# A decoder trunk on one core: rows of each norm split between two engines, the memory's load and norm put in among the first projections

## What is computed

```python
mem_n = rms_norm(mem, mem_norm)               # 256 x 1024, once
for l in range(2):
    h = rms_norm(x, norm_mix[l])
    p = h @ w_in[l]                           # one wide projection for three mixers
    ...                                       # RWKV-7, gated DeltaNet, sparse MLA
    x = x + (g_a * y_a + g_b * y_b + g_c * y_c) @ w_mix_out[l]
    x = x + memory_xattn(rms_norm(x, norm_xattn[l]), mem_n, ...)
    h = rms_norm(x, norm_ffn[l])
    x = x + (swiglu(h, ...) if l == 0 else moe_swiglu(h, router, ...))
return rms_norm(x, final_norm)

def rms_norm(x, g):
    return x * rsqrt(mean(x * x, -1) + eps) * g
```

## Time and profile before

| | us |
|---|---|
| three runs, median | 3019.67 |
| three runs, lowest and highest | 3012.88, 3020.87 |
| profiled execution, own time | 3020.0 |
| profiled execution, span of the core | 3017.8 |
| PE busy | 2599.6 |
| DVE busy | 1691.3 |
| ACT busy | 1452.7 |
| mean granted clock of TensorE | 0.949 |

### The profile page before, as it was taken

The page is one execution under the profiler, slowest core; times in us unless marked ns, Lnnn a source line. Parts: engine busy times, 40 slices in busy tenths (PEclk is TensorE's granted clock), DMA queues, the critical chain, the costliest instruction groups (busy, mean ns, idle before and its releaser), DMA issues.

```text
span 3017.8 us, 67151 instructions
## 1 busy us (share of the span) xinstructions
PE 2599.6 (86%) x29799; PEld 2135.1 (71%) x29818; DVE 1691.3 (56%) x1990; ACT 1452.7 (48%) x1904; POOL 353.8 (12%) x180
## 2 busy tenths in 40 slices
PE   6988888899788989888988997878888888888887
PEld 5766666777466768666756875657787788878876
DVE  2445453234215532545542343149999989999996
ACT  2233343233224321433343323248887878888785
POOL 0000001000000000000010000002322322332231
PEclk9999999999999999899989999989999999999999
DMA  5401030133217634211120232249999999999994
GB/s 183 147 29 57 21 94 29 37 101 105 94 56 256 205 105 136 71 43 30 57 70 23 80 109 84 98 175 385 373 354 363 363 354 368 357 362 365 354 366 183
DMA packets 304032, 531.34 MB, mean 176 GB/s; under 512 B 18528, under 2 KB 145760, under 8 KB 303360
## 3 DMA queue, kind: packets, MB, share of 16 engines
q1 hardware_dynamic: 303600, 525.99, 50.4%
q10 hardware_dynamic: 144, 1.05, 0.1%
HBM read 524.91 MB, written 2.10 MB: 175 GB/s over the span
## 4 chain that ended last, share of the span: by engine, by line
PE 64%; DVE 16%; ACT 12%; issue 7%; DMA 0%; ACTq 0%; POOL 0%; DVEq 0%; SPq 0%
PE bank L797 11%; PE bank L698 9%; DVE arena L2680 8%; PE bank L1368 6%; PE bank L1385 4%; PE bank L768 4%; PE bank L1268 4%; PE bank L1227 4%; ACT arena L1989 4%; PE bank L763 3%; PE bank L716 2%; PE bank L642 2%; PE bank L1412 2%; PE bank L1284 2%; DVE yacc L2688 2%
## 5 line engine op out<-in xcount | busy, mean ns | idle before, releaser
L2680 DVE TENSOR_TENSOR arena<-ring,arena 128x2048 bf16<-128x2048 f32 x336 | 813.9, 2441 | 81.9 <-ACT arena L1989 81.9
L1989 ACT ACTIVATE arena<-ring 128x2048 bf16<-128x2048 f32 x336 | 630.4, 1907 | 0.0
L1368 PE MATMUL bank<-arena 128*128 128x0 bf16 x10752 | 489.0, 209 | 42.8 <-DVE arena L2680 32.6
L1368 PEld LDWEIGHTS bank<-arena 128*128 128x128 bf16 x10752 | 478.7, 99 | 49.0 <-DVE arena L2680 35.7
L797 PE MATMUL bank<-feat,ring 128*128 128x256 f32 x1664 | 436.6, 401 | 8.4 <-ACT ring L1554 2.3
L1518 POOL TENSOR_TENSOR arena<-yacc,arena 128x512 bf16<-128x512 f32 x112 | 296.5, 2647 | 1060.2 <-ACT arena L2012 1060.2
L797 PEld LDWEIGHTS bank<-feat,ring 128*128 128x128 f32 x1664 | 310.0, 197 | 88.2 <-issue 43.5
L1385 PEld LDWEIGHTS bank<-arena 128*128 128x128 bf16 x5376 | 254.9, 102 | 15.8 <-issue 10.5
L1385 PE MATMUL bank<-arena 128*128 128x0 bf16 x5376 | 260.2, 212 | 1.2 <-DVE arena L2680 1.1
L698 PE MATMUL bank<-feat,ring 128*128 128x256 f32 x1056 | 230.7, 381 | 5.8 <-issue 5.8
L698 PEld LDWEIGHTS bank<-feat,ring 128*128 128x128 f32 x1056 | 201.6, 191 | 34.7 <-issue 7.1
(11 more groups left out here) (353 smaller groups left out, 3382.1 us busy)
## 6 DMA issues: line engine op xcount, KB each, us to landing
ring<-in_moe_w_gate SPq DMA_DIRECT2D x112, 1024.0 KB, 7.0
ring<-in_moe_w_up SPq DMA_DIRECT2D x112, 1024.0 KB, 6.5
ring<-in_moe_w_down SPq DMA_DIRECT2D x112, 1024.0 KB, 7.0
ring<-in_w_in SPq DMA_DIRECT2D x76, 1024.0 KB, 5.2
ring<-in_xa_w_kv SPq DMA_DIRECT2D x16, 1024.0 KB, 5.4
ring<-in_ffn_w_gate SPq DMA_DIRECT2D x11, 1024.0 KB, 5.3
ring<-in_ffn_w_up SPq DMA_DIRECT2D x11, 1024.0 KB, 5.4
ring<-in_ffn_w_down SPq DMA_DIRECT2D x11, 1024.0 KB, 6.9
```

The lines of the kernel that those rows point to most:

```text
L1368: m = mm(o, w[k // 4][wi][:, k % 4, col:col + P], xg[:, e % 2, xi, k, :].shape_from_register(width[e % 2]), start=i == 0 and k == 0, stop= ...
L1989: sc.activation(w_parts[b][0], ring[:, b * FFN_SLOT:(b + 1) * FFN_SLOT], ACT.Copy).then_inc(S["w_hi"], 1)
L2680: v.tensor_tensor(w_parts[b][1], ring[:, b * FFN_SLOT:(b + 1) * FFN_SLOT], w_parts[b][0], ALU.subtract).then_inc(S["w_lo"], 1)
```

## The change

It has three parts.

Each of the seven norms whose result is turned now splits the scaling: ACT writes `xn` for `t` = 0 (a Copy with the row's factor as its scale), DVE only for `t` = 1. PE turns the eight blocks of half 0 once ACT's is done, and then the eight of half 1. A bank is full when its last block of half 1 is in. The final norm is as it was.

The loads are in another order: `mem` is issued behind the second chunk of `w_in`, `rout` behind the fourth and with a semaphore of its own, for which PE waits only at the router (L1318 of the changed kernel). ACT, DVE and PE wait at the start for `par` and `cs` alone.

The memory's norm is taken from the start and put behind the first two chunks (four tiles) of layer 0's projections, on all three engines. PE does not wait there for its eight results, but later, behind the twelfth chunk.

```diff
@@ SP
             sp.dma_start(par[:, :, :], params.rearrange("l p n -> p l n")).then_inc(S["par_dma"], 16)
-            sp.dma_start(yacc[...], mem...).then_inc(S["mem_dma"], 16)
             sp.dma_start(xt[:, :, :], x.rearrange("(a p) d -> p a d", p=P)).then_inc(S["in_dma"], 16)
             sp.dma_start(cs[:, :], consts).then_inc(S["par_dma"], 16)
-            sp.dma_start(rout[:, :, :], rows(router)).then_inc(S["par_dma"], 16)
...
                 for i, ch in enumerate(mix_chunks(l)):
+                    if not l and i == 2:
+                        sp.dma_start(yacc[...], mem...).then_inc(S["mem_dma"], 16)
+                    if not l and i == MIX_SLOTS:
+                        sp.dma_start(rout[:, :, :], rows(router)).then_inc(S["rout_dma"], 16)
@@ PE
-            def norm():
-                pe.wait_ge(S["norm_xn"], c.need("norm_xn", 2))
-                for b in range(4):
-                    for k in (2 * b, 2 * b + 1):
-                        for t in range(TT):
-                            m = tr(bk(4 + b, (k % 2) * 256 + t * P, P), xn[:, t, k * P:(k + 1) * P])
-                            if not k and not t:
-                                release(m)
-                            if k % 2 and t == 1:
-                                m.then_inc(S["norm_T"], 1)
-                pe.wait_ge(S["feat_ready"], c.need("feat_ready", 4))
-                pe.wait_ge(S["feat_half"], c.need("feat_half", 4))
+            def norm(used=True):
+                for t, done in enumerate(("norm_x0", "norm_xn")):
+                    pe.wait_ge(S[done], c.need(done))
+                    for k in range(KT):
+                        m = tr(bk(4 + k // 2, (k % 2) * 256 + t * P, P), xn[:, t, k * P:(k + 1) * P])
+                        if not k and not t:
+                            release(m)
+                        if k % 2 and t == 1:
+                            m.then_inc(S["norm_T"], 1)
+                if used:
+                    pe.wait_ge(S["feat_ready"], c.need("feat_ready", 4))
+                    pe.wait_ge(S["feat_half"], c.need("feat_half", 4))
...
-                proj_chunks(12, feat)
+                if l:
+                    proj_chunks(12, feat)
+                else:
+                    proj_chunks(2, feat)
+                    norm(False)
+                    proj_chunks(10, feat)
+                    pe.wait_ge(S["feat_ready"], c.need("feat_ready", 4))
+                    pe.wait_ge(S["feat_half"], c.need("feat_half", 4))
...
             def moe_route():
+                pe.wait_ge(S["rout_dma"], 16)
...
-            pe.wait_ge(S["par_dma"], c.need("par_dma", 48))
-            norm()
+            pe.wait_ge(S["par_dma"], c.need("par_dma", 32))
@@ ACT
+                act.wait_ge(S["norm_r"], c.need("norm_r"))
+                act.wait_ge(*c.last())
+                sc.activation(xn[:, 0, :], src[:, 0, :], ACT.Copy, scale=small[:, 6:7]).then_inc(*c.inc("norm_x0"))
...
                     evac(raw[:, n % 4, 3:259])
+                    if not l and n == 3:
+                        act.wait_ge(S["mem_dma"], 16)
+                        norm(yflat.rearrange("p (a b) -> p a b", a=TT), "mem_norm", 0, memf)
...
-            act.wait_ge(S["par_dma"], 48)
+            act.wait_ge(S["par_dma"], 32)
             sc.activation(small[0:1, 78:79], par[0:1, 0, 0:1], ACT.Copy).then_inc(*c.inc("act_step"))
-            act.wait_ge(S["mem_dma"], 16)
-            norm(yflat.rearrange("p (a b) -> p a b", a=TT), "mem_norm", 0, memf)
@@ DVE
-                for t in range(TT):
+                for t in range(TT) if final else (1,):
...
                     v.scalar_tensor_tensor(dst, dst, pc(l, "mu", n), raw[:, n % 4, 3:259], ALU.mult, ALU.add).then_inc(*c.inc("raw_free"))
+                    if not l and n == 3:
+                        dve.wait_ge(S["mem_dma"], 16)
+                        norm(yflat.rearrange("p (a b) -> p a b", a=TT), "mem_norm", 0, memf)
```

More of the change, by code:

```diff
@@ L89 @@
 SEMS = ("in_dma par_dma mem_dma wl_dma slot0 slot1 slot2 slot3 slot4 slot5 weights_used "
-        "dve_step act_step norm_ss norm_ms norm_sd norm_xn norm_T feat_ready feat_half x_new "
+        "dve_step act_step norm_ss norm_ms norm_sd rout_dma norm_xn norm_x0 norm_r norm_T feat_ready feat_half x_new "
         "proj_full proj_evac raw_free gate_sig rkv_ready vlow_full vlow vres_full vres_sig vres_done "
@@ L548, in _ @@
             sp.dma_start(par[:, :, :], params.rearrange("l p n -> p l n")).then_inc(S["par_dma"], 16)
-            sp.dma_start(yacc[:, :, :].rearrange("p a b -> p (a b)").rearrange("p (a d) -> p a d", a=TT),
-                         mem.rearrange("(a p) d -> p a d", p=P)).then_inc(S["mem_dma"], 16)
             sp.dma_start(xt[:, :, :], x.rearrange("(a p) d -> p a d", p=P)).then_inc(S["in_dma"], 16)
             sp.dma_start(cs[:, :], consts).then_inc(S["par_dma"], 16)
-            sp.dma_start(rout[:, :, :], rows(router)).then_inc(S["par_dma"], 16)
             def load(chunk, slots, rounds=0):
@@ L592, in _ @@
                 for i, ch in enumerate(mix_chunks(l)):
+                    if not l and i == 2:
+                        sp.dma_start(yacc[:, :, :].rearrange("p a b -> p (a b)").rearrange("p (a d) -> p a d", a=TT),
+                                     mem.rearrange("(a p) d -> p a d", p=P)).then_inc(S["mem_dma"], 16)
+                    if not l and i == MIX_SLOTS:
+                        sp.dma_start(rout[:, :, :], rows(router)).then_inc(S["rout_dma"], 16)
                     if i == MIX_SLOTS:
@@ L624, in _ @@
             load_moe(down_chunks(NE * STEPS - 1, NE - 1))
-            sp.wait_ge(S["norm_xn"], 2 * (2 + 3 * LAYERS))
+            sp.wait_ge(S["norm_xn"], 1 + 3 * LAYERS + TT)
             sp.dma_start(out.rearrange("(a p) d -> p a d", p=P),
@@ L2133, in norm @@
                 dve.wait_ge(S["norm_sd"], c.need("norm_sd"))
-                v.reciprocal(small[:, 6:8], small[:, 4:6]).then_inc(*c.inc("dve_step"))
+                v.reciprocal(small[:, 6:8], small[:, 4:6]).then_inc(*c.inc("dve_step" if final else "norm_r"))
                 dve.wait_ge(*c.last())
-                for t in range(TT):
+                for t in range(TT) if final else (1,):
                     if final:
                         if t == 0:
-                            dve.wait_ge(S["par_dma"], 64)
+                            dve.wait_ge(S["par_dma"], 48)
                         v.scalar_tensor_tensor(yflat[:, t * D:(t + 1) * D], src[:, t, :], small[:, 6 + t:7 + t],
@@ L2749, in moe @@
                 dve.wait_ge(S["mo_x"], 4 * NE)
-            dve.wait_ge(S["par_dma"], 48)
-            dve.wait_ge(S["mem_dma"], 16)
-            norm(yflat.rearrange("p (a b) -> p a b", a=TT), "mem_norm", 0, memf)
+            dve.wait_ge(S["par_dma"], 32)
             dve.wait_ge(S["in_dma"], 16)
```

## The result

The changed kernel takes 3024.14 us (median of 22 runs) against 3019.55 for the kernel before (median of 22 runs beside them): ratio 1.0017, 95% interval 1.0011 to 1.0024. It is slower by 0.17%, 4.6 us. One of the 22 executions of the changed kernel took 10095.91 us; the ratio leaves it out, and without it the median is 3024.07. The prediction was 3018.9 us, 0.75 faster, with a range of 3011 to 3025. The time lies inside the range, but on the other side of the kernel before, and the interval does not reach down to 1. The forecast of a small gain was wrong.

The account below looks back on a forecast made before the run. Bound: the opening's chain of loads and norms until 34 us, then PE. Terms -3.0 - 9.35 + 10.1 + 0.3 + 1.2 = -0.75 took the median of 3019.67 to 3018.9 us, range 3011 to 3025.

Parts of the forecast that it names:

- What bounds the kernel: Opening: up to 34 us the chain of loads and norms bounds, behind it PE, so savings there reach the end.
- Part 1, the loads: Opening: without the memory's load ahead, the constants land sooner and ACT's first instruction starts at 10.2 us; -3.0 us.
- Parts 2 and 3, the memory's norm: Leaving the opening saves 9.35 us; returning behind the fourth projection tile costs 10.1, with PE idle 6.2; together +0.75.
- Part 4, the halves: Six norms waited for: first transpose 0.38 us earlier, later evacuations give 0.44 back; +0.3 us in all, bounds -0.7 to +0.5.
- Part 5, the clock: First projections: the new 6.2 us idle stretch drops PE to half clock; +1.2 us.
- slower, by the clock: Rival: clock stays low behind the idle stretch before tile five, and the first tile is cold; +4.8, 3024.5 us; chance 0.15.
- It does hide: Rival: the memory's xn is ready when PE comes, so PE pays only the transposes; -8.5, 3011.2 us; chance 0.03.
- The halves pay: Rival: the 0.38 us saved by split scaling stays in all seven norms; -3.4, 3016.3 us; chance 0.14.
- The constants land no earlier: Rival: in the opening w_in's chunks share the engines with cs, so the loads gain nothing; +2.2, 3021.9 us; chance 0.08.
- The rule on idle gaps: Skill's rule, applied at the projections: an idle gap amid matrix work returns PE to half clock; kept the +1.2 us.

Follow-up runs that it names:

- e_move: The changed kernel with every norm scaling both halves on DVE and turning bank by bank, as before; 3019.07 us, ratio 1.0002 to the kernel before.
- halves_fill: e_halves plus two unneeded f32 matmuls between last transpose and wait for evacuations in each norm PE waits for; 3018.35 us, ratio 0.9993.
- before_fill: The kernel before plus two unneeded f32 matmuls in each of the seven norms PE waits for; 3018.05 us, ratio 0.9993.
- e_halves: The kernel before with only the split scaling and the transposes half by half; 3030.89 us, ratio 1.0044.
- e_bank: The changed kernel with PE waiting for both halves and turning bank by bank, as before; 3015.43 us, ratio 0.9991 to the kernel before.
- e_hidden_move: e_move with the memory's transposes behind six projection tiles in place of four; 3010.50 us, ratio 0.9972 to the kernel before.
- e_hidden_bank_fill: e_bank with the memory's transposes behind six tiles in place of four, plus two unneeded matmuls per norm PE waits for; 3008.83 us, ratio 0.9970.

## Why the prediction was wrong, point by point

- **What bounds the kernel** held: in the opening the chain of loads and norms, behind it PE.
- **Part 1, the loads**: -3.0 forecast, -3.5 in the first profile (9.78 against 13.26) and -2.9 in the second (10.34).
- **Parts 2 and 3, the memory's norm**: the idle stretch was forecast at 6.2 us and is 6.11, the transposes at 3.6 and are 3.44. The fifth tile's evacuation is 1.5 and 1.6 us ahead in the two profiles. `e_move` gives -0.1 us for parts 1 to 3 with their clock; the sum of those terms without the halves' 0.3 was -1.05, or -0.67 with the 0.38 that the unsplit scaling puts back into the idle stretch (6.50 us there). All lie inside the interval of 0.9993 to 1.0011.
- **Part 4, the halves: the step that failed.** The Copy takes 1.15 us, as forecast. DVE's evacuations start 3.33 us behind PE's first transpose in the opening, as forecast, where it was 2.90, and 2.69 at layer 0's cross attention, where it was 2.50. In the opening the norm's end moved as forecast, the first projection starting 6.79 us behind the reciprocal's end in place of 6.76, and at the cross attention it is 6.06 in place of 6.28. So the steps of the norm were right or nearly so, and `halves_fill`, 0.3 us over `before_fill`, agrees with "+0.3 us for six norms" as far as its interval of 2.7 us either way can tell. (Six times 0.06 are 0.36; the sum took 0.3.) What was wrong is to end the term there. I costed the norm up to its last evacuation, and the price lies in the tile behind it: 3.05 us at each cross attention, and some 4.6 us behind the router's start. By itself the part costs 11.7 us (`e_halves`), and 4.7 on top of the other parts (the changed kernel's 4.6 less `e_move`'s -0.1; the unchanged stretch, 3.4 us quicker there than in `e_move`, hides a part), against bounds of -0.7 to +0.5. The order of the transposes is what costs: with the split but the old order (`e_bank`) the kernel is 8.7 us faster than as changed.
- **Part 5, the clock**: I looked for the clock's price only at the new idle stretch in the opening. There the +1.2 has the right size and no fixed place: in the first profile the fifth tile, from first matmul to evacuation, takes 3.70 us but the first one 5.42, in the second the fifth takes 4.56 and the first 3.73. The change alters six more idle gaps, and the trace of before showed where to look: both norms ahead of the cross attentions have a fall to 0.50 that ends just before the projection, and layer 1's first norm has one that doesn't. "Transposes hardly feel it" was wrong too. It compared 3.65 with 3.50 us, both in the opening, where the views print 1.00. Transposes that come straight from dense work take 1.91 us (`e_hidden_move`), and those at a granted 0.50 throughout 3.68 (layer 1's first norm), so both had been slow ones. The clock's record begins only at 32.2 us in the trace of before, and a view prints 1.00 where there is no record. The opening's 1.00 is no evidence of a full clock.
- **The rivals**: "slower, by the clock" (0.15) has the right side and size (+4.8 forecast, +4.6 measured) and the wrong place: it blamed the stretch in the projections and the first tile; `e_move` shows that these cost nothing net. So its agreement in size is luck. "It does hide" did not come true, as PE waited 6.11 us. "The halves pay" did not come true for the change as it is; and where `e_bank`, with the old order of the transposes, is 3.6 us under `e_move`, 3.4 of them lie in unchanged code. "The constants land no earlier" did not come true.
- **The rule on idle gaps**, which I weighed only for the new idle stretch, bears on the norms' gaps as well (the Trainium skill, TensorE: Matmul & The Clock Gate, section on HAM oscillation): the burst behind the gap of 1.83 us starts at half clock, and with the gap filled it doesn't.

## What to carry to other kernels

When an edit makes a burst of matrix work shorter, or moves it ahead of an idle gap, cost the work behind the gap as well: read the granted clock in the gap and the length of the first tile behind it. The gap's length alone does not tell: behind 1.40 us the tile took 3.73 us in one kernel and 5.30 in another. Where PE must wait for an evacuation, a matmul or two that nobody needs can be cheaper than idling; test it, because it also tells whether the clock is the cause. It is no sure gain: it gave 11.2 us in the changed kernel, and 0.5 us in `e_hidden_bank_fill`. And look at stages that the edit doesn't touch before you add up single gains. And an engine whose instructions run in order starts a "side" job only where it stands in its queue: put the consumer a tile or two later, and the wait is hidden.

## What the runs showed of the hardware that I had not expected

- The same 16 transposes (f32, 128 x 128) take 1.91 us straight behind dense work, and 2.41 to 3.68 us behind an idle stretch of 3.99 us or more.
- 0.43 us more of idle time and 0.25 us less of work between the same two bursts made the first tile 3.05 us longer; with the idle time as before (`e_bank`) it was 1.6 us longer. 1.56 us of unneeded matmuls in the gap brought it back to 3.73 us.
- The same 1418 matmuls of unchanged code took 189.1 us in one version and 186.2 in another, at a mean clock of 0.92 and 0.93.
- The granted clock is shown as 1.00 up to its first record in an execution (32.2 us in the kernel before), while the transposes there, 3.32 to 3.65 us, run about as slowly as at 0.50 (3.68).
- Two matmuls per norm that nobody needs make the changed kernel 11.2 us faster; without the halves it is 2.5 us, which the interval does not tell from nothing.
